# A hybrid attention kernel: the dilated branch takes two token blocks in each step, and a barrier, the log gates, the sparse shares and the statistics stand in other places

## The reference, cut to what matters

```python
def dilated_attention(q, k, v, slopes):            # branch C, 12 heads in 3 groups of 4
    for g, (window, dilation) in enumerate(((128, 1), (512, 4), (2048, 16))):
        ...                                        # query t attends to t - j*dilation, j*dilation <= window
        lse = logsumexp(logits); p = exp(logits - lse); o = p @ v
    alpha = softmax(stack(lses), axis=0)           # share of each group, by softmax denominators
    return concatenate([alpha[g] * outs[g] ...])
...
log_f = log_sigmoid(fa + b_forget)                 # branch A: forgetting attention
c = cumsum(log_f);  logit[t, s] += c[t] - c[s]
...
merged = sigmoid(ga) * ((A * silu(za)) @ w_a) + sigmoid(gb) * ((B * silu(zb)) @ w_b) + sigmoid(gc) * ((C * silu(zc)) @ w_c)
return rmsnorm(x + merged @ w_o)
```

## Time and profile before

| | |
|---|---|
| time, median of 3 runs | 1410.93 us (1410.43 to 1411.33) |
| profiled execution: time | 1410.6 us |
| profiled execution: span from first to last instruction | 1408.8 us |
| PE busy | 1380.7 us, 98% of the span |
| DVE busy | 734.6 us, 52% |
| ACT busy | 694.6 us, 49% |
| chain of work that ended last | PE 93%, DVE 2%, ACT 2%, issue 1%, DMA 1% |
| branch C | about 136 to 409 us of the span |
| its statistics and the first z tile | about 409 to 431 us |
| branch A, branch B | about 643 to 873 us, 873 to 1138 us |

### The profile page before, as it was taken

How to read it: one execution, slowest core, us unless ns; L and a number is a source line. 1 busy time by engine, 2 the same in 40 slices (tenths; PEclk the granted TensorE clock), 3 DMA queues, 4 the chain that set the end, 5 groups by cost and what they waited for, 6 DMA issues and landing times.

```text
span 1408.8 us, 21178 instructions
## 1 busy us (share of the span) xinstructions
PE 1380.7 (98%) x7962; PEld 1111.4 (79%) x7962; DVE 734.6 (52%) x1658; ACT 694.6 (49%) x1522; POOL 104.0 (7%) x203
## 2 busy tenths in 40 slices
PE   7999999999998999999999999999999999999998
PEld 6987777777777888887778777777777778888886
DVE  6568666666656785564343444634333345222634
ACT  7467777767753351114545565554454523112323
POOL 3133000000002100000000001100000020000000
PEclk9999999999999999999999999999999999999999
DMA  6154111111113322213212122212232142222522
GB/s 217 28 140 117 32 34 35 38 39 31 32 37 94 103 74 76 82 60 98 57 27 61 25 67 67 86 38 61 83 90 61 53 144 67 74 84 68 168 94 105
DMA packets 111124, 103.76 MB, mean 74 GB/s; under 512 B 9712, under 2 KB 95088, under 8 KB 110768
## 3 DMA queue, kind: packets, MB, share of 16 engines
q1 hardware_dynamic: 97824, 58.22, 15.4%
q0 software_dynamic: 13200, 44.20, 9.9%
HBM read 82.06 MB, written 16.14 MB: 70 GB/s over the span
## 4 chain that ended last, share of the span: by engine, by line
PE 93%; DVE 2%; ACT 2%; issue 1%; DMA 1%; SPq 0%; POOL 0%; ACTq 0%; DVEq 0%; POOLq 0%
PE bank L967 22%; PE bank L969 22%; PE bank L968 22%; PE bank L1125 7%; PE bank L1144 6%; PE slot L1115 6%; PE slot L967 2%; PE slot L968 2%; PE slot L969 2%; PE slot L1080 1%; PE bank L1091 1%; PE bank L985 0%; DVE hs L1555 0%; DMA iq_st<-iq_hl 0%; DMA pw_raw<-in_w_in_dram 0%
## 5 line engine op out<-in xcount | busy, mean ns | idle before, releaser
L967 PE MATMUL bank<-hs,w_hl 128*128 128x512 f32 x1088 | 436.3, 401 | 5.8 <-DVE tm L1802 5.4
L969 PE MATMUL bank<-hs,w_hl 128*128 128x512 f32 x1088 | 425.7, 391 | 0.0
L968 PE MATMUL bank<-hs,w_hl 128*128 128x512 f32 x1088 | 424.9, 391 | 0.0
L1520 DVE TENSOR_TENSOR w_hl<-w_raw,w_hl 128x512 fp32r<-128x512 f32 (+1 forms) x168 | 113.8, 679 | 263.4 <-ACT w_hl L1225 261.9
L967 PEld LDWEIGHTS bank<-hs,w_hl 128*128 128x128 f32 x1088 | 205.2, 189 | 47.0 <-issue 7.8
L969 PEld LDWEIGHTS bank<-hs,w_hl 128*128 128x128 f32 x1088 | 204.8, 188 | 44.7
L968 PEld LDWEIGHTS bank<-hs,w_hl 128*128 128x128 f32 x1088 | 205.5, 189 | 39.0
L1225 ACT ACTIVATE w_hl<-w_raw 128x512 fp32r<-128x512 f32 (+1 forms) x168 | 103.9, 620 | 153.3 <-PE bank L969 145.4
L1547 DVE TENSOR_SCALAR_CACHE_REDUCE idle_out<-score,state 128x768 uint8<-128x768 f32 (+3 forms) x140 | 115.4, 824 | 4.8
L1716 DVE CUSTOM_DVE_ANT_0 slot<-slot,score 128x128 f32<-128x128 f32 (+7 forms) x64 | 47.4, 782 | 70.7 <-PE slot L1115 70.7
L1421 ACT ACTIVATE idle_out<-score,state 128x896 bf16<-128x896 f32 x64 | 70.2, 1098 | 11.7 <-DVE state L1543 10.3
(11 more groups left out here) (324 smaller groups left out, 2233.3 us busy)
## 6 DMA issues: line engine op xcount, KB each, us to landing
w_raw<-in_w_in_dram SPq DMA_DIRECT2D x136, 256.0 KB, 2.8
merged_scratch<-ms POOLq DMA_DIRECT2D x16, 512.0 KB, 3.5
ms<-merged_scratch POOLq DMA_DIRECT2D x16, 512.0 KB, 3.9
xn<-in_x_dram SPq DMA_DIRECT2D x8, 512.0 KB, 6.1
iq_st<-iq_hl POOLq DMA_DIRECT2D x32, 128.0 KB, 2.8
w_raw<-in_w_o_dram SPq DMA_DIRECT2D x16, 256.0 KB, 3.4
share_b<-share_scratch_c POOLq DMA_DIRECT2D x24, 128.0 KB, 2.8
negc<-cum_scratch POOLq DMA_DIRECT2D x6, 512.0 KB, 5.0
```

The source lines that it names most:

```text
L967: pe.matmul(out_, wh, mh, start=start, stop=False)
L968: pe.matmul(out_, wh, ml, start=False, stop=False)
L969: return pe.matmul(out_, wl, mh, start=False, stop=stop)
L1520: v.tensor_tensor(lo, src, hi.bitcast(F32), ALU.subtract).then_inc(w_low, 1)
```

## The change

Branch C is now attended in "runs" of two neighbouring token blocks: `pair_run` takes lists of units, and in branch C a list has two. The logits of both units go to one slot (`col` is the column where a unit starts), both units' `pv` go to one bank in two column ranges with one claim, and the transposes of both units are grouped by four together. There are 24 steps instead of 48, a `pick` in each, and `pump` is called with twice the pieces (3.2 instead of 1.6 in channels 1 to 4, 2.5 in channel 0, 2.75 in channel 5). The buffer of the probabilities of branch C moves to `share_b`, so the `c_merge` barrier moves ahead of `share_turn`. `gates` and `gate_sums` move into the merge of branch C, behind the first piece of the z tiles 3 and 5. The statistics' transposes get a piece after the second and after the third group, one more piece stands ahead of `share_turn`. At the end of branch B, `share_turn` moves three pieces earlier, ahead of the barrier.

```diff
-    def pair_run(units, before, rate):
+    def pair_run(runs, before, rate):
...
             def logits():
-                x = units[s]
-                x["slots"] = 2 if x["W"] > HALF else 1
-                x.update(S=nxt("S", x["slots"]), L=nxt("L", 2), unit=nxt("unit"))
-                units_seen.append(x)
-                plan.append(("logits", x))
+                run, wide = runs[s], sum(x["W"] for x in runs[s])
+                slots = 2 if wide > HALF else 1
+                first_S, first_L, col = nxt("S", slots), nxt("L", 2 * len(run)), 0
+                for k, x in enumerate(run):
+                    x.update(slots=slots, S=first_S, L=[first_L + k, first_L + len(run) + k], col=col,
+                             last=x is run[-1], run=run, held=runs[s - 1][0] if s else None)
+                    col += x["W"]
+                    units_seen.append(x)
+                    plan.append(("logits", x))
...
             if s >= 2:
-                units[s - 2]["pv"] = ring()
-                plan.append(("pv", units[s - 2]))
+                pv = ring()
+                for x in runs[s - 2]:
+                    x["pv"] = pv
+                    plan.append(("pv", x))
             if 1 <= s <= n:
-                x = units[s - 1]
-                parts = [(hh, c) for hh in range(2) for c in range(x["W"] // P)]
-                x["groups"] = [dict(parts=parts[g0:g0 + 4]) for g0 in range(0, len(parts), 4)]
+                parts = [(x["b"], hh, c) for x in runs[s - 1] for hh in range(2) for c in range(x["W"] // P)]
+                groups = [dict(parts=parts[g0:g0 + 4]) for g0 in range(0, len(parts), 4)]
...
             if s < n:
-                plan.append(("exp", units[s]))
-                if units[s]["br"] == "c" and s % 2 == 1:
+                plan.append(("exp", runs[s][-1]))
+                if runs[s][0]["br"] == "c":
                     pick()
...
             elif x["br"] == "c" and x["ch"] in (0, NCH["c"] - 1):
-                pump(1.25 if x["ch"] == 0 else 1.375)
+                pump(many * (1.25 if x["ch"] == 0 else 1.375))
             else:
-                pump(2 * rate)
+                pump(many * 2 * rate)
...
-            if br == "c" and ch == 0:
-                before.setdefault(2, []).append(lambda: step("gates"))
-                before.setdefault(4, []).append(lambda: step("gate_sums", u=[ring(), ring()]))
...
     step("phase", name="c_stats")
+    defer[0] = True
     for g in range(3):
         for half in range(2):
             step("stat_turn", g=g, half=half, use=ring())
+        if g:
+            pump(1)
+    step("stat_back", use=ring())
     pump(1)
-    step("stat_back", use=ring())
-    defer[0] = True
-    pump(2)
+    step("phase", name="c_merge")
+    pump(1)
     share_turns("c")
-    next(fill[0])
     defer[0] = False
-    step("phase", name="c_merge")
     flush_later()
...
+        if b["kind"] == "zc" and b["c"] >= 3 and a["th"] == 0 and b["base"] == 0:
+            if b["c"] == 3:
+                step("gates")
+            if b["c"] == 5:
+                step("gate_sums", u=[ring(), ring()])
...
+    share_turns("b")
     flush()
     step("phase", name="b_merge")
     fill.append(merge("b"))
-    pump(2)
-    share_turns("b")
     flush()
...
-        PR = {"c": at(52, "pc", [P, 2, 2 * P]), "a": at(28, "pa", [P, 2, T]), "b": at(32, "pb", [P, 2, T])}
+        PR = {"a": at(28, "pa", [P, 2, T]), "b": at(32, "pb", [P, 2, T])}
...
+        PR["c"] = share_b[:, 0:2, :]
...
                 elif kind == "pv":
-                    for grp in a["groups"]:
-                        freed(pe, grp["use"])
-                    if a["br"] != "b":
-                        freed(pe, tiles["V" + a["br"], a["ch"], 1])
-                    claim(pe, a["pv"])
+                    if a["col"] == 0:
+                        for grp in a["groups"]:
+                            freed(pe, grp["use"])
+                        if a["br"] != "b":
+                            freed(pe, tiles["V" + a["br"], a["ch"], 1])
+                        claim(pe, a["pv"])
```

More of the change, by code:

```diff
@@ L201, in pick @@
             step(kind, n=n)
-    def pair_run(units, before, rate):
-        n = len(units)
+    def pair_run(runs, before, rate):
+        n = len(runs)
         defer[0] = True
@@ L211, in logits, with turn @@
             def logits():
-                x = units[s]
-                x["slots"] = 2 if x["W"] > HALF else 1
-                x.update(S=nxt("S", x["slots"]), L=nxt("L", 2), unit=nxt("unit"))
-                units_seen.append(x)
-                plan.append(("logits", x))
-            def turn(x, groups):
-                for g in x["groups"][groups]:
+                run, wide = runs[s], sum(x["W"] for x in runs[s])
[7 more added lines that the diff above has]
+                    plan.append(("logits", x))
+            def turn(run, groups):
+                for g in run[0]["groups"][groups]:
                     g.update(use=ring(), tp=nxt("tp"))
-                    unit_of_tp.append(x)
-                step("turn", unit=x, groups=groups)
-            between = s < n and s >= 1 and units[s - 1]["W"] > HALF
+                    unit_of_tp.append(run[0])
+                step("turn", unit=run[0], groups=groups)
+            between = 1 <= s < n and runs[s - 1][0]["slots"] == 2
             if s < n and not between:
@@ L265, in attend @@
     def attend(br, after):
-        units, before = [], {}
+        runs, before = [], {}
         for ch in range(NCH[br]):
@@ L288, in attend @@
                 W = {0: P * min(b + 1, 2), 1: P * (b % 2 + 1), 2: P}[ch // 2] if br == "c" else P * (b + 1)
-                units.append(dict(br=br, ch=ch, b=b, W=W))
-        pair_run(units, before, 0.8)
+                x = dict(br=br, ch=ch, b=b, W=W)
+                if b % 2 and br == "c":
+                    runs[-1].append(x)
+                else:
+                    runs.append([x])
+        pair_run(runs, before, 0.8)
     def qkv(br, ch, parts=1):
@@ L436, in build_plan @@
     share_turns("a")
-    pair_run([dict(br="b", ch=ch, b=b, W=(b + 1) * P) for ch in range(NCH["b"]) for b in range(TB)], {}, RATE_B)
+    pair_run([[dict(br="b", ch=ch, b=b, W=(b + 1) * P)] for ch in range(NCH["b"]) for b in range(TB)], {}, RATE_B)
+    share_turns("b")
     flush()
@@ L1304, in _ @@
                         full(act, u)
-                        A(f_raw[:, half * HALF:(half + 1) * HALF], bank[u[0]][0:A_HEADS, :], ACTF.Copy,
+                        A(f_cum[:, half * HALF:(half + 1) * HALF], bank[u[0]][0:A_HEADS, :], ACTF.Copy,
                           scale=-1.0).then_inc(bank_free[u[0]], 1)
@@ L1384, in _ @@
                 elif kind == "exp":
-                    if a["unit"]:
-                        full(act, units[a["unit"] - 1]["groups"][-1]["use"])
+                    if a["held"] is not None:
+                        full(act, a["held"]["groups"][-1]["use"])
                     for hh in range(2):
-                        act.wait_ge(logit_ready, a["L"] + hh + 1)
-                        mx, dn = stats_of(a, hh)
-                        ins = A(PR[a["br"]][:, hh, 0:a["W"]], slot_of(a, hh)[1], ACTF.Exp, bias=mx, scale=-1.0, accum_out=dn)
+                        act.wait_ge(logit_ready, a["L"][hh] + 1)
+                        for x in a["run"]:
+                            mx, dn = stats_of(x, hh)
+                            ins = A(PR[x["br"]][:, hh, x["col"]:x["col"] + x["W"]], slot_of(x, hh)[1], ACTF.Exp, bias=mx,
+                                    scale=-1.0, accum_out=dn)
                         if hh or a["slots"] == 2:
```

82 lines of the change are left out of this document (46 added, 36 removed).

## The result

The changed kernel takes 1415.8 us (median of 12 runs, 1411.83 to 1416.61), the kernel before 1410.78 (12 runs beside them, 1409.11 to 1416.13). The ratio is 1.003, 95% interval 1.002 to 1.0039: slower by 5.0 us, where 5.0 were forecast. The profiled execution took 1415.18 us, span 1413.4, against 1410.6 and 1408.8 before.

A forecast was written before the change was run, and what follows sets the result against it. PE, busy 1380.7 of 1408.8 us, was taken to bound the kernel. -11.3+4.6+14.4+3.0-3.8-3.1+1.2 = +5.0 on the profiled 1410.6 gave 1415.6 us (own range 1412 to 1422; with rivals 1400 to 1426).

The forecast's parts named there:

- Larger groups, -11.3: Branch C on PE: pairing blocks makes fewer, larger matmul groups, saving 0.52 or 0.37 us a run, 11.3 us in all.
- Rival 4: The larger groups in branch C save PE nothing: 1427 us; chance 0.07.
- The shared bank, +4.6: Branch C: the second group of transposes waits for ACT to copy pv from their shared bank, 4.6 us.
- The readers, +14.4: Branch C: PE waits because ACT's and DVE's reads of q and k banks come late, behind the threshold round; 14.4 us.
- rival 1: The q and k readers in branch C are in time, or late by a few tenths: 1398 us; chance 0.18.
- rival 2: Reader stalls at half size, 7 us, no clock lost: 1405, or about 1411 with the shared bank's high side; chance 0.16.
- the ring's term: Branch C: PE's second transposes wait for the bank shared with pv; 4.6 us, upper bound 12.
- The clock in branch C, +3.0: PE's granted clock falls twice behind the reader stalls in branch C, 1.5 us each, 3 us in all.
- Rival 3: The clock falls at every reader stall in branch C, costing 13.5 us instead of 3: 1426 us; chance 0.07.
- The gates, -3.8: PE's waits behind the gates, 0.47 and 1.81 us, and 1.5 for the clock go: 3.8 us saved.
- The statistics and the z tile, -3.1: First z tile of branch C: PE's 4.4 us stall becomes 2.7; with clock and statistics' transposes, 3.1 us saved.
- The end of branch B, +1.2: The 1.02 us wait at branch B's merge goes, but PE waits about 2.2 us for the reciprocal: 1.2 us lost.

The follow-up runs named there:

- e4: The kernel before, with only the gates and `gate_sums` moved into branch C's merge, blocks not paired: 1407.34 us, ratio 0.998.
- e6: e5 with the statistics and first z tile of branch C back in the order of the kernel before: 1402.5 us, ratio 0.9942.
- e5: The changed kernel with the edits of e1 and e2 together: 1398.61 us, ratio 0.9914.
- e9: e7 with one token block in each step of branch C, not paired, as before the change: 1401.33 us, ratio 0.9928.
- e7: e5 with the transposes of branch C's shares one piece earlier, ahead of the piece behind the barrier: 1396.21 us, ratio 0.9897.
- e1: The changed kernel with branch C's threshold round issued behind the readers of the next channel's first small q and k piece: 1399.89 us, ratio 0.9927.
- e2: The changed kernel with the last transposes of branch B's shares back where they stood before the change: 1414.35 us, ratio 1.0019.
- e10: e7 with pv of branch C's channels 0 to 3 issued between the first and second group of transposes: 1394.96 us, ratio 0.9884.
- e3: The changed kernel with pv of branch C's channels 0 to 3 issued between the two groups of transposes: 1415.11 us, ratio 1.0033.
- e8: The changed kernel, order kept, with ACT's two threshold-round counts reading only half their columns (thresholds differ): 1407.26 us, ratio 0.9971.

## Why the prediction was right, step by step

The forecast was 1415.6, the median is 1415.8. The parts, measured one by one, give the same. Gates -3.3 (e4), statistics -3.9 (e6 against e5), two blocks in a step with timely readers -5.1 (e9 against e7), readers behind the round +15.9 (e1), the end of B +1.4 (e2): +5.0. Each is a difference of two medians that may be off by about 1 us, so the exactness of the sum is chance. That it comes near 5 is in part built in, since most of these kernels stand on one chain of single steps (before, e4, e9, e7, e5, e1, the changed kernel), and such steps must add up. What is tested freely are two of them: the statistics, -3.6 along the chain (e4 to e9, less what e7 has over e5) and -3.9 by e6, and the end of B, 1.3 along the chain and 1.4 by e2.

- **Larger groups, -11.3.** The steps bear it out. Two steps took 3.10 and one more entry and exit of 0.17; one now takes 2.95, of which 0.17 is the bank: 0.49 saved, forecast 0.52. By places branch C is 3.7 longer; the readers' 15.8 less the gates' 4.7 (2.28 of waits, 1.5 of clock, 0.96 of transposes) would make 11.1, which leaves -7.4 for the groups and the shared bank together, and e9 gives 5.1 + 2.3 = 7.4 too. The forecast had 6.7. Rival 4 (they save nothing) is out. The sign that PE's busy time in branch C would fall by about 11 came out at 9.0 (269.9 to 260.9).
- **The shared bank, +4.6.** Six transposes would take 0.41 and two times 0.11 (the earlier trace rows has eight at 1.10, four at 0.66), 0.63; they took 1.00 in channels 2 and 3. Eight would take 0.85 and took 1.02. 8 x 0.17 + 7 x 0.37 = 4.0. Right as a cost; but e10 shows that only about 1.4 of it can be had by this other order. The page TensorEngine Tiling (Key Properties) of the Trainium skill says that a change of mode drains the engine. The 0.18 of e3 is in line with it; no run here isolates it.
- **The readers, +14.4.** Nine waits, 13.7 us: in channel 1 1.55 and 2.11 where 1.7 and 2.2 were forecast, in channel 2 1.34 and 1.70 where 1.3 and 1.8 were, and the last one 1.05 where 1.0 was. With what a wait costs beyond its listed idle time it is 15.8, 1.4 more than forecast. e1 and e8 show the cause, the round in ACT's queue. This was rival 1's and rival 2's question. Rival 1's time, 1398, is what e1 measures within 2 us: the kernel in which the readers are in time. Rival 2's other time is added up wrongly in the prediction: with the ring's term at 12 it would be 1412.6, not about 1411, still no change.
- **The clock in branch C, +3.0.** Mis-sized in the two profiles of the changed kernel: no fall there. But a fall is not a fixed property of a wait. Behind the same 2.1 us at 209 it fell in the profiles of e2 and e3 and not in the two of the changed kernel. The twelve spans stand in groups, 1410.0, 1411.4 (two), 1412.8 to 1413.5 (three), 1414.5 to 1414.8 (six), 1.4 apart, and the two profiles with two falls lie at 1413.0 and 1413.4. By places one fall costs 1.6 (e2 in C, e1 at the end of B). Read so, an estimate, the six longest runs have a third fall, and the median lies between them and the next group. That this third one is in C is not shown, as no such run was profiled. Rival 3 (one at each of the nine) is out: no profile has more than two in C.
- **The gates, -3.8.** Measured -3.3. In e4's profile branch C is 4.7 shorter, the 0.96 us of `gate_sums`' transposes among it, and the merge behind it 1.2 longer.
- **The statistics and the z tile, -3.1.** The wait is 2.32, forecast 2.7. By places the profile gave -1.6, and 0.96 of the difference is the transposes moved here: -2.6. By e6 the part is worth -3.9.
- **The end of branch B, +1.2.** The mis-sized term. The wait was 1.97, forecast 2.2 (the prediction's own terms add up to 2.05), but I priced no slower clock behind it; there was one, in both profiles. By places +2.3. The 1.0 that went with the old wait is right.

So the clock's term was put at the wrong places: two in C and half a one at the z tile, 2.5 falls or 3.75 us, where the profiles have one at the z tile and one at the end of B. What I left out at B, about 1.5, and what the readers cost beyond the forecast, 1.4, stand against the 3.0 that I put too much in C. They cancel. This is the part of the agreement that was luck.

The order of e10_values_between, with the same pairs of blocks, takes 1394.96 us where the kernel before took 1411.54 in that batch: 1.16% less by the ratio (0.98 to 1.33%), and faster than both kernels.

## What to carry to other kernels

When steps are merged to save group changes on the busy engine, count what each in-order queue of the other engines now has between the last use of a buffer and its read, not their busy share: ACT was 49% busy and cost 14 us. Place long work that nobody waits for, here a threshold round of 2.45 us, behind the reads that free a bank, not ahead of them. And test such a term by size as well as by order: here the wait shrank by what the suspect shrank (0.77 for 0.79), where the change of order had moved DVE's work too. Where runs of one kernel differ by whole falls of the clock, compare places in two profiles, with the granted clock beside them, and not the medians alone: that is how e3's 1.4 us is seen.

## What was not expected of the hardware

- The spread between runs goes with the waits. Kernels with a wait of 2 us or more in mid-program spread over 1.0 us (e6) to 4.8 us (the changed kernel, in steps of 1.4), the kernel before over 2.8 and, with its one run of 1416.13, over 7.0; those without such a wait over 0.24 (e9), 0.45 (e7) and 0.44 (e10), in four or five runs each.
- After the same wait the clock falls in one run and holds in the next. Behind the wait for the reciprocal, 1.97 us in five profiles, it fell in three (both of the changed kernel, and e3) and held in two (e1, e8). Behind the wait for kc, 2.1 us in four, it fell in two (e2, e3).
- Half the columns on ACT are not half the time: the count of 1024 columns took 1.15 us, of 512 0.72, of 896 1.06, of 448 0.69.
- Four transposes cost 0.18 us more with a matmul group of another shape behind them (0.59) than with a piece (0.41), in e3.
